# Converting, multiplying and releasing weights in half units of two k-tiles

## What is computed

```python
for i in range(DEPTH):                      # 4
    mod = c_act @ ada_w[i] + ada_b[i]       # 1024 x 6144: shifts, scales and gates
    h = modulate(rms_norm(x, norm_gain[i, 0]), sh1, sc1)
    y = mixer_i(h)                          # stick-breaking, MoBA, sliding window, stick-breaking
    x = x + g1 * y
    h = modulate(rms_norm(x, norm_gain[i, 1]), sh2, sc2)
    x = x + g2 * ((silu(h @ w_gate) * (h @ w_up)) @ w_down)     # 1024 -> 2816 -> 1024
x_new = x + gt1 * merge(y_attn, o_dl, dz, ga, gd)               # final block
x_new = x_new + gt2 * (square(relu(hm @ w_mlp1)) @ w_mlp2)      # 1024 -> 4096 -> 1024
```

## Time and profile before

| | |
|---|---|
| runs, us | 2117.68, 2118.93, 2123.82 |
| median, us | 2118.93 |
| span of the profiled execution, us | 2113.7 |
| mean granted TensorE clock | 0.972 |
| TensorE, weight loads, VectorE, ScalarE, GpSimd busy, us | 1926.3, 1500.4, 1342.8, 917.3, 112.5 |
| read from HBM, mean | 390.17 MB, 185 GB/s |

### The profile page before, as it was taken

The page is one execution under the profiler, slowest core; times in us unless marked ns, Lnnn a source line. Parts: engine busy times, 40 slices in busy tenths (PEclk is TensorE's granted clock), DMA queues, the critical chain, the costliest instruction groups (busy, mean ns, idle before and its releaser), DMA issues.

```text
span 2113.7 us, 33128 instructions
## 1 busy us (share of the span) xinstructions
PE 1926.3 (91%) x13890; PEld 1500.4 (71%) x13890; DVE 1342.8 (64%) x1412; ACT 917.3 (43%) x1367; POOL 112.5 (5%) x139
## 2 busy tenths in 40 slices
PE   4888999999899998899999898998999888798999
PEld 3666887655687764687777677777777777776877
DVE  6776775563587734588755578875537645366465
ACT  3555444332544334544355554435435321335443
POOL 1001000110100000100000100001000302000000
PEclk9998999999999999999999999998989999999999
DMA  8763886564599931599933367983123000234552
GB/s 321 287 224 116 277 284 238 202 209 144 186 338 313 334 104 60 169 338 316 343 112 122 116 201 257 320 307 131 58 86 120 2 4 4 83 111 150 172 185 102
DMA packets 215401, 393.37 MB, mean 186 GB/s; under 512 B 11337, under 2 KB 130133, under 8 KB 199893
## 3 DMA queue, kind: packets, MB, share of 16 engines
q1 hardware_dynamic: 214741, 391.12, 54.0%
q0 software_dynamic: 512, 0.13, 0.0%
HBM read 390.17 MB, written 1.05 MB: 185 GB/s over the span
## 4 chain that ended last, share of the span: by engine, by line
PE 57%; DVE 24%; ACT 10%; issue 6%; DMA 2%; POOL 0%; DVEq 0%; ACTq 0%; SPq 0%; POOLq 0%
PE G L2161 12%; PE G L2163 11%; PE G L2162 11%; DVE w_lo L1443 11%; PE G L2367 6%; DVE acc L1496 5%; ACT w_hi L939 5%; PE G L2462 2%; PE A L2756 2%; ACT full L1004 1%; PE G L2770 1%; DMA raw<-in_ffn_w_down 1%; DVE act_st L1781 1%; PE A L2768 1%; DVE n_st L1553 1%
## 5 line engine op out<-in xcount | busy, mean ns | idle before, releaser
L1443 DVE TENSOR_TENSOR w_lo<-raw,w_hi 128x2048 fp32r<-128x2048 f32 (+2 forms) x237 | 513.4, 2166 | 285.4 <-ACT w_hi L939 274.8
L939 ACT CAST w_hi<-raw 128x2048 fp32r<-128x2048 f32 (+1 forms) x230 | 427.7, 1860 | 532.7 <-PE G L2163 479.8
L2161 PE MATMUL G<-w_hi,h_hi 128*128 128x512 f32 (+2 forms) x1232 | 491.3, 399 | 29.6 <-DVE w_lo L1443 12.1
L2163 PE MATMUL G<-w_hi,h_lo 128*128 128x512 f32 (+2 forms) x1232 | 480.9, 390 | 0.0
L2162 PE MATMUL G<-w_lo,h_hi 128*128 128x512 f32 (+2 forms) x1232 | 480.6, 390 | 0.0
L1496 DVE SCALAR_TENSOR_TENSOR acc<-raw,c_col,acc 128x2048 f32<-128x2048 f32 x120 | 282.0, 2350 | 43.3 <-DMA raw<-in_ada_w 22.5
L2161 PEld LDWEIGHTS G<-w_hi,h_hi 128*128 128x128 f32 x1232 | 235.0, 191 | 85.1 <-issue 40.0
L2163 PEld LDWEIGHTS G<-w_hi,h_lo 128*128 128x128 f32 x1232 | 234.1, 190 | 49.3
L2162 PEld LDWEIGHTS G<-w_lo,h_hi 128*128 128x128 f32 x1232 | 235.4, 191 | 45.1
L2161 PE MATMUL G<-w_hi,act_hi 128*128 128x512 f32 (+2 forms) x624 | 243.8, 391 | 24.0 <-DVE w_lo L1443 21.6
L2163 PE MATMUL G<-w_hi,act_lo 128*128 128x512 f32 (+2 forms) x624 | 241.0, 386 | 0.0
(11 more groups left out here) (402 smaller groups left out, 2097.4 us busy)
## 6 DMA issues: line engine op xcount, KB each, us to landing
raw<-in_ada_w SPq DMA_DIRECT2D x96, 1024.0 KB, 5.1
raw<-in_ffn_w_gate SPq DMA_DIRECT2D x88, 512.0 KB, 4.0
raw<-in_ffn_w_up SPq DMA_DIRECT2D x88, 512.0 KB, 5.1
raw<-in_ffn_w_down SPq DMA_DIRECT2D x40, 1024.0 KB, 5.2
raw<-in_w_mlp SPq DMA_DIRECT2D x32, 1024.0 KB, 5.3
raw<-in_w_ada SPq DMA_DIRECT2D x24, 1024.0 KB, 5.4
raw<-in_w_in SPq DMA_DIRECT2D x18, 1024.0 KB, 5.3
raw<-in_sb_w_in SPq DMA_DIRECT2D x32, 512.0 KB, 4.8
```

Source lines behind the costliest of these rows:

```text
L939: nc.scalar.copy(w_hi[:, c % 2, 0:len(kts), 0:n], raw[:, slot].rearrange("p (k n) -> p k n", k=UNIT_K)[:, 0:len(kts), 0:n])\
L1443: return nc.vector.tensor_tensor(w_lo[:, c % 2, ks, 0:n], raw[:, slot].rearrange("p (k n) -> p k n", k=UNIT_K)[:, ks, 0:n], w_hi[:, c % 2, ...
L2161: nc.tensor.matmul(banks[t][:, 0:n], x_hi[:, kt, ts], w_hi[:, u % 2, i, 0:n], start=st, stop=False)
L2163: ins = nc.tensor.matmul(banks[t][:, 0:n], x_lo[:, kt, ts], w_hi[:, u % 2, i, 0:n], start=False, stop=en)
```

## The change

Casts, low parts, products and release go by half units of two k-tiles. `w_hi` and `w_lo` are cut into four half buffers in the same memory, half hc in buffer hc % 4. A table (`first_half`, `half_done_at`) numbers the halves over all converted units; a unit of two k-tiles is one half. `gemm_done` now counts each half's last product, and the places that wait for whole units use `done_at`. The products go half by half over both token tiles, except where `by_tile` or `tiles` keeps the old order (first unit after a norm, last unit before one). `raw_free` is gone: SyncE and GpSimd wait for `lo_ready`, `acc_done` or `accc_done` themselves, and VectorE's waits for its own instructions ahead of the increments go.

```diff
-        w_hi = w_hi_t[:, :].rearrange("p (s k n) -> p s k n", s=2, k=UNIT_K)
+        w_hi = w_hi_t[:, :].rearrange("p (s k n) -> p s k n", s=2 * HALVES, k=HALF_K)
...
+        first_half, half_done_at, done_at = {}, [], [0]
+        for u, x in enumerate(units):
+            if x[0] == "native":
+                done_at.append(done_at[-1] + 1)
+                continue
+            first_half[u] = len(half_done_at)
+            half_done_at += [done_at[-1] + j + 1 for j in halves_of(u)]
+            done_at.append(half_done_at[-1])
...
+                elif s >= RING and loads[s - RING][0] == "unit":
+                    sp.wait_ge(lo_ready, low_parts(unit_of[s - RING]))
                 elif s >= RING:
-                    sp.wait_ge(raw_free, freed_by_dve(s - RING + 1))
+                    sp.wait_ge(acc_done, nth_ada[s - RING] + 1)
...
                 act.wait_ge(landed[slot], count)
-                if c >= 2:
-                    act.wait_ge(gemm_done, converted[c - 2] + 1)
-                nc.scalar.copy(w_hi[:, c % 2, 0:len(kts), 0:n], raw[:, slot].rearrange("p (k n) -> p k n", k=UNIT_K)[:, 0:len(kts), 0:n])\
-                    .then_inc(hi_ready, 1)
+                for j in halves_of(u):
+                    hc = first_half[u] + j
+                    if hc >= 2 * HALVES:
+                        act.wait_ge(gemm_done, half_done_at[hc - 2 * HALVES])
+                    nc.scalar.copy(w_hi[:, hc % (2 * HALVES), :, 0:n], landed_half(slot, j)[:, :, 0:n]).then_inc(hi_ready, 1)
...
-                        dve.wait_ge(accc_done, n + 1)
-                    dve.wait_ge(acc_done, k.a)
-                    dve.sem_inc(raw_free, 1)
...
+                steps = [(t, j) for t in range(NT) for j in parts] if by_tile or tiles else [(t, j) for j in parts for t in range(NT)]
+                for t, j in steps:
+                    hc = first_half[u] + j
+                    if t == 0:
+                        pe.wait_ge(hi_ready, hc + 1)
+                        pe.wait_ge(lo_ready, hc + 1)
...
+                    if t == NT - 1 and done is gemm_done:
+                        k.ins.then_inc(gemm_done, 1)
```

More of the change, by code:

```diff
@@ L1440, in link, with convert_half @@
                 dve.wait_ge(dve_step, chain[0])
[L1442 to L1460, removed]
-                dve.sem_inc(raw_free, 1)
-            def convert_half(half):
-                if half == 0:
+            def convert_half(j):
+                if j == 0:
                     k.u += 1
@@ L2146, in wait_panel_free, with unit @@
                     pe.wait_ge(free_act if who == "act" else free_dve, count)
[L2148 to L2150 removed]
+            def unit(x_hi, x_lo, kts, banks, first, last, n=512, done=gemm_done, ready=None, tiles=False, by_tile=False):
+                u = k.u
                 k.u += 1
[L2152 to L2167 removed]
@@ new lines, in unit, with half_products @@
+                if done is part_done:
+                    k.ins.then_inc(part_done, 1)
+            def half_products(u, j, t, x_hi, x_lo, kts, bank, first, last, n=512):
+                at = (first_half[u] + j) % (2 * HALVES)
+                ts = slice(t * P, t * P + P)
+                ks = kts[HALF_K * j:HALF_K * j + HALF_K]
+                for i, kt in enumerate(ks):
+                    nc.tensor.matmul(bank, x_hi[:, kt, ts], w_hi[:, at, i, 0:n], start=first and i == 0, stop=False)
+                    nc.tensor.matmul(bank, x_hi[:, kt, ts], w_lo[:, at, i, 0:n], start=False, stop=False)
+                    k.ins = nc.tensor.matmul(bank, x_lo[:, kt, ts], w_hi[:, at, i, 0:n], start=False, stop=last and i == len(ks) - 1)
@@ L2504, in _ @@
                     for h in range(2):
[L2505 removed]
+                        unit(h_hi, h_lo, range(4 * h, 4 * h + 4), G[2 * (pn % 2):2 * (pn % 2) + 2], h == 0, h == 1, ready=ready_at(f_h, h),
+                             by_tile=p == 0 and h == 0)
                         if h == 0 and p >= 1:
@@ L2627, in _ @@
                     done = gemm_done if not both else part_done if h else None
-                    unit(h_hi, h_lo, kts, banks[0], h == 0, h == 1, n, done, ready=ready_at(f_x, h))
+                    unit(h_hi, h_lo, kts, banks[0], h == 0, h == 1, n, done, ready=ready_at(f_x, h), by_tile=pi == 0 and h == 0)
                     for step, s in LAT_SLOTS.get(2 * pi + h - 0.5, []):
@@ L2913, in _ @@
                     for h in range(2):
-                        unit(h_hi, h_lo, range(4 * h, 4 * h + 4), G[2 * (pn % 2):2 * (pn % 2) + 2], h == 0, h == 1, ready=ready_at(f_h, h))
+                        unit(h_hi, h_lo, range(4 * h, 4 * h + 4), G[2 * (pn % 2):2 * (pn % 2) + 2], h == 0, h == 1, ready=ready_at(f_h, h),
+                             by_tile=part == 0 and p == 0 and h == 0)
                         if h == 0 and p >= 1:
```

103 lines of the change are left out of this document (47 added, 56 removed).

## The result

The changed kernel takes 2042.4 us (median of four runs) against 2120.0 for the kernel before on the same chip: a ratio of 0.963, with a 95% interval of 0.9605 to 0.9655. Predicted were 2083, so the direction was right and the gain was twice what was forecast: 78 us and not 36, beyond the fast end of the range (2061). The profiled execution took 2044.7 us with a span of 2042.9, against 2113.7 before: 70.8 us less between two profiled executions.

A forecast was written before the change was run, and what follows sets the result against it. TensorE was taken to set the pace, its waits for conversions being the gain. Terms 12.3 + 11.0 + 7.0 + 3.0 + 1.5 + 4.4 - 3.0 made 36 us, so 2118.9 became 2083, range 2061 to 2101.

The forecast's parts named there:

- (f): TensorE's eight hid_st waits and small act_st waits: 3.4 plus 1.0 us gained as VectorE's preceding low part ends sooner.
- No self-waits: VectorE no longer waits for its own low part and sum: 0.30 us saved wherever it has work waiting.
- (c): Gate and up panels of the last block, waits for w_lo and act_st of 9.1 us: 7.0 us gained.
- (a): Unit after a down projection's half-size unit: seven TensorE waits of 1.75 us all go, 12.3 us gained.
- (b): Two stick-breaking mixers, w_lo and "issue" waits of 13.5 us: 9.2 plus 1.8 of slow clock, 11.0 us gained.
- (d): Five waits in down projections where the cast had waited for a DMA, 9.0 us: a third, 3.0 us, gained.
- (e): Longest w_lo wait, 3.3 us, in the final block behind VectorE's head norm: 1.5 us gained.
- Against: Losses deducted: 1.0 us in norms and 2.0 us that the second and third block give back to DMA.
- DMA takes it back: Feed-forwards, DMA 90 to 92% busy: TensorE may not run ahead; gain only 21 us, 2098; chance 0.22.
- Freeing VectorE brings nothing: VectorE instructions after removed self-waits start no sooner, so the split only costs there: gain 25.5 us, 2093; chance 0.06.
- No earlier start: Loads or queue order hold the first half as long as the whole: within 5 us of before, 2116; chance 0.06.
- Slower: Each of some 230 added half boundaries stops TensorE, 0.25 us each: 21 us slower, 2140; chance 0.04.

The follow-up runs named there:

- e11: Kernel before with only the split of cast and low part into two instructions each; half-size units use two half buffers: 2087.5 us, ratio 0.9838.
- e5: Changed kernel with start, release, product order and VectorE self-waits as before; split, SyncE's direct waits and smaller buffer use stay: 2064.9 us, ratio 0.9753.
- e9: Kernel of e5 with SyncE's direct wait undone too: VectorE raises a count behind its self-wait and SyncE waits for that: 2080.9 us, ratio 0.9817.
- e13: Kernel of e11, but VectorE starts the first half's low part only when ScalarE has cast both halves: 2141.3 us, ratio 1.0098.
- e2: Changed kernel, but TensorE waits for all halves of a unit before its first product: 2047.0 us, ratio 0.9671.
- e16: Kernel of e10, but VectorE still raises the old count behind its self-waits, though nothing waits for it: 2118.7 us, ratio 0.9999.
- e7: Kernel before, in whole units, without VectorE's self-waits and count; SyncE waits for low part and sums directly: 2092.3 us, ratio 0.9883.
- e12: Kernel of e5 without VectorE's self-waits (changed kernel with start, release and product order of before): 2059.3 us, ratio 0.9723.
- e1: Changed kernel with VectorE's waits for its own results put back, without the count: 2045.4 us, ratio 0.9660.
- e14: Changed kernel with VectorE's self-waits, and SyncE waiting for VectorE's count behind them, as before: 2060.4 us, ratio 0.9712.
- e6: Changed kernel, but half-size units of a down projection use up two half buffers: 2040.5 us, ratio 0.9631.
- e15: Changed kernel with each weight load as two half-size DMAs, the first issued behind the first half's low part: 2043.9 us, ratio 0.9637.
- e10: Kernel before, in whole units, with SyncE's direct waits alone; VectorE keeps its self-waits: 2105.4 us, ratio 0.9928.
- e0: The changed kernel itself, run again beside its variants: 2039.4 us, ratio 0.9625.
- e17: Changed kernel without waits that others imply: VectorE waits only for the half's cast, TensorE only for its low part: 2040.9 us, ratio 0.9629.
- e8: Changed kernel in quarters of one k-tile, eight buffers, casts and low parts of 512 columns: 2039.6 us, ratio 0.9621.

## Why the prediction was half right

Three steps failed. The sum took the waits' idle time for the whole cost of a stop; it put the two instructions for one at a small cost and no gain, where they gain 34 us (e11); and it put SyncE's direct wait at nothing, though the same edit frees VectorE of an instruction worth 13.6 us (e5 against e9).

**What bounds it** held. TensorE sets the pace and the waits for the conversions were what could be gained. Of its idle time 51.9 us went (span less busy: 187.4 before, 135.5 after).

**The sum of brackets**, of the idle times in front of TensorE's instructions, failed first. The span fell by 70.8 us, 18.9 more than the idle time, because TensorE's busy time fell as well, and of this only some 2 us of slow clock stood in my sum. The rows around 332.69 above show the main reason. From the product at 330.54 to the next it is 2.15 us instead of 0.23, and the one after starts 0.30 later: 1.99 us are lost where the bracket says 1.75, since a matmul's modelled end lies 0.16 us behind the start of its follower. A stop shorter than that has no bracket. In the kernel before, at a panel's transposes:

```profile
263.78 0.39 PE L2163 MATMUL G<-w_hi,h_lo 128*128 128x512 f32 x1
264.09 0.44 PE L2497 MATMUL A<-consts,act_st 128*128 128x128 f32 x2
```

0.31 us from start to start, no wait shown. In the changed kernel:

```profile
212.27 0.39 PE L2183 MATMUL G<-w_hi,h_lo 128*128 128x512 f32 x1
212.50 0.60 PE L2509 MATMUL A<-consts,act_st 128*128 128x128 f32 x4
```

0.23. Over the 44 panels these intervals sum to 21.6 us before (a median of 0.315) and 11.7 after (0.230): 9.9 us from a wait of which the earlier trace rows show 6.2, and of which term (f) took 1.0. The eight hid_st waits: 6.6 us start to start before, 1.8 after, 4.8 gained against the 3.4 taken and the 3.5 in brackets. The rest of the 18.9 is in part the clock: (1 - 0.972) x 2113.7 = 59 us lost to it before and (1 - 0.973) x 2042.9 = 55 now, at most 4 us. How all of it divides was not worked out.

**The cost of the split** was the step with the wrong sign. I charged it 0.15 us of VectorE and 0.19 us of ScalarE per unit and saw the overlap only as part of TensorE's earlier start. It is a gain of its own, 34 us (e11), and 55 us lie between the kernels with the overlap and without (e13). In e11 the waits for w_lo and "issue" still come to 23.2 + 4.9 us, only 14 less than before; the rest of the 34 I put down to work behind the low part on VectorE, such as act_st, and to what the brackets leave out. That was not shown by place. The earlier start of TensorE, my main step, is worth 10 us when removed and, with release and order, 20 on top of the rest. Where conversions end 0.8 us sooner and VectorE has its time back, TensorE seldom reaches a unit before all of it is there: it waits 10.5 us for conversions in e2, 42.5 before.

**No self-waits:** the 0.30 us per place was right for most places, its cause was not. 0.1 to 0.2 is the instruction that raises the count, 0.1 the wait. "SyncE issues each load a little sooner" was costed at nothing, and that is right (e16); what I overlooked is that the same edit takes an instruction from VectorE. The two are worth 25 us alone (e7) and 20 with the split (e9 against e12), where (c) took 7. The Trainium skill (VectorE: DVE Perf Modes, The DRAIN you can't avoid) found that eight copies with a semaphore after each took no longer than with one after the last. This does not carry over to a wait for the predecessor and a count of its own: VectorE starts 0.12 us later in e1 and 0.34 in e14 than in the changed kernel. An increment that the instruction itself carries stood in all kernels, and no run shows its cost.

**By terms:** (a) all seven waits went, as said, but not through the buffer (e6). (b) 11.0 for the two mixers, measured 21.5 for both stages as a whole: of 13.5 us for w_lo and "issue" one wait of 1.2 is left, so the 3.2 us that I held back as given back to the softplus steps did not show; stops cost more than their brackets, and the clock brought up to 4.7 where I took 1.8. (c) 7.0; the last feed-forward as a whole gave 17.3. (d) 3.0 of 9.0, for fear of the DMA: it went to 330 and 355 GB/s, and of 33.7 + 8.8 us for w_lo and "issue" 6.2 are left where I forecast 14. I had also misread three of the five waits (1.2, 1.6 and 1.2 us). They come at the end of a down projection, where no DMA holds the low part but VectorE's residual. One of 1.4 is left. The first of them in the kernel before:

```profile
727.54 1.91 ACT L939 CAST w_hi<-raw 128x2048 fp32r<-128x2048 f32 x1 [3.52 <-PE G L2163]
730.47 1.30 DVE L1607 TENSOR_TENSOR x_res<-x_res,n_st 128x512 f32<-128x512 f32 x2
731.68 2.28 DVE L1443 TENSOR_TENSOR w_lo<-raw,w_hi 128x2048 fp32r<-128x2048 f32 x1
734.11 0.47 PE L2161 MATMUL G<-w_hi,act_hi 128*128 128x512 f32 x1 [1.23 <-DVE w_lo L1443]
```

The cast had ended at 729.45, and the low part began when VectorE was done with x_res. Only the two waits of 2.5 us in the last block stood behind a late load; 0.4 and 0.9 us are left there. The casts now stand 78.9 us for in_ffn_w_down instead of 41.9, and TensorE notices no more of it than these 1.3 us. (e) 1.5; the wait fell from 3.3 to 2.3. **Against:** the 1.0 for norms was not seen, h_lo fell by 2.2.

**Rivals.** DMA takes it back: no, the feed-forwards gained most, and e15 changes nothing. Freeing VectorE brings nothing: the opposite. No earlier start: no. Slower: not in this change, since the half boundaries cost nothing; but e13 is 21 us slower with the same two instructions, where VectorE waits for both casts and nothing else of the change is in.

What stays open is how the 20 us of start, release and order divide: each was only taken out of the full change or all three together, and singly they come to 15. Why VectorE's freed time reaches the span at the rate it does was not taken apart by place either, nor how much of the gain the clock made.

## What to carry to other kernels

Two engines that work on the same buffer one after the other can gain from a split into halves even when the consumer waits for the whole: compare what the pair takes from first start to last end (here 4.24 and 3.44 us), not the busy time added. Let the producer's own instruction raise the semaphore that others wait for; an instruction that only raised a count took 0.1 to 0.2 us of VectorE at every use here, though no row of the profile counts it as busy. And sum a pipelined engine's losses from start to start: with the 512-column matmuls of this kernel the brackets leave out 0.24 us of each stop and all of a stop under 0.16. Compare the granted clock of both kernels as well: here it rose from 0.970 to 0.975 as the waits went.

## What the runs showed of the hardware

VectorE's next start lies 0.15 to 0.25 us behind its predecessor's end where it waits for the predecessor and raises a count in between (before, e14, e16); 0.03 with the wait alone (e1, e10); -0.08 with neither (e7, the changed kernel). Raising the count costs 11 to 15 us in this kernel at some 350 uses, one per low part and per sum (e10, e5 against e9, e1 against e14), and not through the loads that wait for it (e16). With fewer waits of TensorE its mean granted clock rose from 0.970 to 0.975 (e0); without the overlap it fell to 0.963 (e13). Some 440 waits per engine that were already met cost nothing measurable (e17), and neither did 0.3 us more of VectorE per unit in quarters (e8).
